# Mixing layer of a two-block model: columns reordered, small steps set between weight chunks, heads taken by pairs

## The reference

```python
def token_mix(x, w_in, w_out, ...):
    h = x @ w_in
    (nq, kc, vc, ks, vs, kw, vw, gl, u, gq, gk, gv, ga, gr) = jnp.split(h, split_pts, axis=-1)
    gates = jax.nn.sigmoid(gl).reshape(B, S, NSA_HEADS, 3)
    o_a = nsa_mixer(...)      # 8 heads of 64: attention over compressed, selected and window keys
    o_b = pool_mixer(u, pool_w, pool_scale)     # trailing means minus token, small product, scale
    o_c = gla_mixer(gq, gk, gv, ga, gr, ...)    # gated linear attention, 4 heads, chunks of 64
    return jnp.concatenate([o_a, o_b, o_c], axis=-1) @ w_out
```

## Time and profile before

| | us |
|---|---|
| median of 3 runs | 2589.47 |
| the runs | 2577.11, 2590.91, 2589.47 |
| the profiled execution, its own time | 2579.11 |
| span of the profiled execution | 2577.3 |
| TensorE busy (share) | 2478.0 (96%) |
| VectorE busy | 1514.1 (59%) |
| ACT busy | 1060.4 (41%) |
| GpSimd busy | 144.2 (6%) |
| mean granted clock of TensorE | 0.975 |

### The profile page before, as it was taken

The page is one execution under the profiler, slowest core; times in us unless marked ns, Lnnn a source line. Parts: engine busy times, 40 slices in busy tenths (PEclk is TensorE's granted clock), DMA queues, the critical chain, the costliest instruction groups (busy, mean ns, idle before and its releaser), DMA issues.

```text
span 2577.3 us, 43010 instructions
## 1 busy us (share of the span) xinstructions
PE 2478.0 (96%) x18918; PEld 2270.4 (88%) x18918; DVE 1514.1 (59%) x2062; ACT 1060.4 (41%) x1321; POOL 144.2 (6%) x174
## 2 busy tenths in 40 slices
PE   8999799999999899999999999999998999999998
PEld 8999579999999589989988989799897998998897
DVE  5456465564564555558655555755666555865654
ACT  4333344333334343336234344443455444633432
POOL 0001000000010000011110000100001000011000
PEclk9999699999999699999999999999999999999999
DMA  7569126556577045554225554455544555422553
GB/s 251 182 188 204 62 77 190 192 180 196 181 187 185 17 139 188 188 152 122 89 100 182 184 174 149 146 180 192 174 159 137 196 182 172 129 84 99 173 194 115
DMA packets 320810, 405.37 MB, mean 157 GB/s; under 512 B 48688, under 2 KB 281232, under 8 KB 320624
## 3 DMA queue, kind: packets, MB, share of 16 engines
q1 hardware_dynamic: 314960, 383.50, 47.2%
q0 software_dynamic: 5664, 19.13, 2.5%
HBM read 401.55 MB, written 1.05 MB: 156 GB/s over the span
## 4 chain that ended last, share of the span: by engine, by line
PE 86%; DVE 6%; ACT 3%; issue 2%; POOL 1%; DMA 1%; SPq 0%; DVEq 0%; POOLq 0%; ACTq 0%
PE ps L416 25%; PE ps L417 25%; PE ps L418 25%; PE ps L2233 2%; PE ps L707 1%; DVE w_lo L410 1%; ACT w_hi L403 1%; PE ps L1049 1%; DVE ws L1289 1%; DMA raw<-in_w_in 1%; DVE ws L1277 1%; PE ps L2275 1%; DVE ws L756 0%; DVE small L760 0%; PE ps L1061 0%
## 5 line engine op out<-in xcount | busy, mean ns | idle before, releaser
L410 DVE TENSOR_TENSOR w_lo<-raw,w_hi 128x2048 fp32r<-128x2048 f32 (+2 forms) x363 | 813.8, 2266 | 153.7 <-ACT w_hi L403 153.3
L403 ACT CAST w_hi<-raw 128x2048 fp32r<-128x2048 f32 (+2 forms) x363 | 685.5, 1889 | 498.0 <-PE ps L418 408.9
L416 PE MATMUL ps<-aT_hi,w_hi 128*128 128x256 f32 x2840 | 807.9, 284 | 0.2 <-DVE w_lo L410 0.2
L417 PE MATMUL ps<-aT_lo,w_hi 128*128 128x256 f32 x2840 | 804.1, 283 | 0.0
L418 PE MATMUL ps<-aT_hi,w_lo 128*128 128x256 f32 x2840 | 804.1, 283 | 0.0
L416 PEld LDWEIGHTS ps<-aT_hi,w_hi 128*128 128x128 f32 x2840 | 543.0, 191 | 5.1 <-DVE w_lo L410 0.4
L417 PEld LDWEIGHTS ps<-aT_lo,w_hi 128*128 128x128 f32 x2840 | 543.1, 191 | 3.7
L418 PEld LDWEIGHTS ps<-aT_hi,w_lo 128*128 128x128 f32 x2840 | 543.0, 191 | 0.5
L416 PE MATMUL ps<-w_hi,h_hi 128*128 128x512 f32 x928 | 363.4, 392 | 5.5 <-DVE h_lo L1566 4.2
L417 PE MATMUL ps<-w_lo,h_hi 128*128 128x512 f32 x928 | 362.4, 390 | 0.0
L418 PE MATMUL ps<-w_hi,h_lo 128*128 128x512 f32 x928 | 361.1, 389 | 0.0
(11 more groups left out here) (364 smaller groups left out, 2082.5 us busy)
## 6 DMA issues: line engine op xcount, KB each, us to landing
raw<-in_mlp_w SPq DMA_DIRECT2D x128, 1024.0 KB, 5.4
raw<-in_ffn_wd SPq DMA_DIRECT2D x44, 1024.0 KB, 4.9
raw<-in_ffn_wg SPq DMA_DIRECT2D x43, 1024.0 KB, 5.3
raw<-in_ffn_wu SPq DMA_DIRECT2D x43, 1024.0 KB, 5.3
raw<-in_gdn_w_in SPq DMA_DIRECT2D x32, 1024.0 KB, 5.7
raw<-in_mlstm_w_in SPq DMA_DIRECT2D x12, 1024.0 KB, 5.4
raw<-in_diff_w_in SPq DMA_DIRECT2D x12, 1024.0 KB, 5.2
raw<-in_w_in SPq DMA_DIRECT2D x8, 1024.0 KB, 5.8
```

The source lines that it names most:

```text
L403: nc.scalar.copy(used_part(hi_slot(n), n), used_part(raw[:, n % RAW, :], n)).then_inc(hi_ready, 1)
L410: nc.vector.tensor_tensor(used_part(lo_slot(n), n), used_part(raw[:, n % RAW, :], n), used_part(hi_slot(n), n).bitcast(F32), ALU.subtract) ...
L416: nc.tensor.matmul(dst, l_hi, r_hi, start=start, stop=False)
L417: nc.tensor.matmul(dst, l_hi, r_lo, start=False, stop=False)
```

## The change

Nothing outside the mixing layer changes. In it:

- **Order of columns.** After values and pool input come GLA keys with gates and decay input (chunk 2), GLA queries and keys (3), raw keys (4), raw values (5), GLA values (6), GLA output gate (7), keys (8), queries (9, 10). The row chunks for pool and GLA outputs come first, the two for head outputs last.
- **Small steps between chunks.** TensorE, ACT and VectorE each have the steps at fixed places: some between the two halves of a chunk, some between chunks. The splits of chunks stand among them.
- **GLA.** The first state is a masked copy, not a sum with a cleared tile; values inside and from before a chunk are summed in one PSUM bank, where a copy and an add stood; ACT takes the squares.
- **Heads by pairs.** scores(f) and values(f) take two heads with their matmuls in turn; ACT copies all 1024 turned columns, and VectorE none; four buffers of probabilities. One row chunk stands before the last transposes, one after the last values; the last two run together as before.

The diff, cut to its core (definitions of the steps that are only moved are left out):

```diff
+                for pieces in ([(NSA_VS, P), (NSA_VW, P)], [(POOL_U, 256)], [(GLA_K, P), (NSA_GATE, 24), (GLA_A, 16)], [(GLA_Q, 256)],
+                               twice(NSA_KC), twice(NSA_VC), [(GLA_V, 256)], [(GLA_R, 256)], [(NSA_KS, P), (NSA_KW, P)],
+                               heads(0), heads(128)):
+                    plan.append(column_pieces(wi, pieces))
...
-                plan += [mixed_row_pieces(wo, 0), mixed_row_pieces(wo, 256), row_pieces(wo, 512), row_pieces(wo, 768)]
+                plan += [row_pieces(wo, 512), row_pieces(wo, 768), mixed_row_pieces(wo, 0), mixed_row_pieces(wo, 256)]
...
+        def pool_means():
+            by_act(1)
+            pe.wait_ge(mix_landed.sem, 16 * MIX_LOADS * (l + 1))
...
+        def scores(f):
+            if f:
+                pe.wait_ge(peaked.sem, peaked.count(l, 2 * f - 1))
+            for k, (keys, more) in enumerate(((k_sel, N_CMP), (k_win, 0))):
+                for t in range(TT):
+                    for g in range(2):
+                        r = slice(64 * g, 64 * g + 64)
+                        o = ps[:, 2 * g + k, (more + P) * t:(more + P) + (more + SEQ) * t]
+                        last = nc.tensor.matmul(o, qT[r, f, t * P:(t + 1) * P], keys[r, 0:more + P * (t + 1)], start=True, stop=True)
...
+        tokens_product(pe, n0 + 2, 2, 168, between=pool_means)
+        by_act(0)
+        features_product(pe, n0 + 3, 0, between=decay_input)
+        pool_outputs()
+        features_product(pe, n0 + 4, 1, between=log_decays)
+        features_product(pe, n0 + 5, 2, between=decay_sums)
+        by_act(2)
+        tokens_product(pe, n0 + 6, 0)
+        compress_hidden()
+        gla_scores()
+        tokens_product(pe, n0 + 7, 1)
+        gla_states()
+        compressed()
+        features_product(pe, n0 + 8, 2)
+        gla_values()
+        features_product(pe, n0 + 9, 0)
+        pe.wait_ge(cmp_set.sem, cmp_set.count(l, 1))
...
+        features_product(pe, n0 + 10, 4, between=first_scores)
+        by_act(6)
+        for f in range(4):
+            if f < 3:
+                scores(f + 1)
+            turned_over(2 * f)
+            if f == 1:
+                gla_output_turned()
+            if f == 3:
+                pe.wait_ge(peaked.sem, peaked.count(l, 7))
+                rows(0, 2)
+            turned_over(2 * f + 1)
+            if f == 2:
+                pe.wait_ge(mixT_lo.sem, mixT_lo.count(l, 1))
+            values(f)
+        rows(1, 3)
...
     def mix_scalar(act, l):
...
+        split_high(act, n0 + 6)
+        act.wait_ge(ga_turned.sem, ga_turned.count(l, 0))
+        act.wait_ge(mix_set.sem, mix_set.count(l, 0))
+        nc.scalar.copy(ga_T[0:16, :], ps[0:16, 3, 0:SEQ]).then_inc(ga_set.sem, 1)
...
+        split_high(act, n0 + 13)
+        exps(0)
+        projected(10)
+        nc.scalar.copy(cols(0, 512, 1024), ps[:, 4, :]).then_inc(mix_act.sem, 1)
+        exps(1)
+        act.wait_ge(pool_scaled.sem, pool_scaled.count(l, 3))
+        output_high(4, pool_y)
+        for f in range(4):
+            copies(2 * f)
...
+            if f < 3:
+                exps(2 * f + 2)
+            copies(2 * f + 1)
+            if f < 3:
+                exps(2 * f + 3)
+            if f == 0:
+                split_high(act, n1 + 3)
...
     def mix_vector(dve, l):
...
+        split_low(dve, n0 + 13)
+        gla_output()
+        peaks(0)
+        peaks(1)
+        for f in range(4):
+            weights(2 * f)
+            if f < 3:
+                peaks(2 * f + 2)
+            weights(2 * f + 1)
+            if f < 3:
+                peaks(2 * f + 3)
+            if f == 0:
+                output_low(0, 4, pool_y)
+                split_low(dve, n1 + 3)
```

More of the change, by code:

```diff
@@ new lines, in log_decays, with decay_sums @@
+        def log_decays():
+            pe.wait_ge(ga_set.sem, ga_set.count(l, 0))
+            for t in range(TT):
+                last = nc.tensor.matmul(ps[:, 4, t * P:(t + 1) * P], ga_T[:, t * P:(t + 1) * P], wa2, start=True, stop=True)
+            last.then_inc(la_pre.sem, 1)
+        def decay_sums():
+            pe.wait_ge(la_set.sem, la_set.count(l, 0))
+            for t in range(TT):
+                s = slice(t * P, (t + 1) * P)
+                nc.tensor.matmul(ps[:, 3, s], la[:, s], consts[:, c_at["upto"]], start=True, stop=True)
+                last = nc.tensor.matmul(ps[:, 3, SEQ + t * P:SEQ + (t + 1) * P], consts[:, c_at["after"]], la[:, s],
+                                        start=True, stop=True)
+            last.then_inc(b_sum.sem, 1)
@@ new lines, in gla_values @@
+        def gla_values():
+            for t in range(TT):
+                for h in range(4):
+                    nc.tensor.matmul(ps[:, 5, t * 256 + 64 * h:t * 256 + 64 * h + 64], att[:, t, h * P:(h + 1) * P],
+                                     gv[:, t, 64 * h:64 * h + 64], start=(t == 0 and h == 0), stop=False)
+            for c in range(1, 4):
+                pe.wait_ge(s_set.sem, s_set.count(l, c - 1))
+                r = slice(64 * (c % 2), 64 * (c % 2) + 64)
+                last = nc.tensor.matmul(ps[r, 5, (c // 2) * 256:(c // 2 + 1) * 256], qtT[:, 64 * c:64 * c + 64], S_gla[:, c, :],
+                                        start=False, stop=c >= 2)
+            last.then_inc(gla_summed.sem, 1)
@@ L1067, in mix_tensor @@
-        for e in range(10):
-            if 1 <= e < 7:
-                scores(e + 1)
-            if 1 <= e <= 8:
-                turned_over(e - 1)
-            if e >= 2:
-                values(e - 2)
-        n1 = start["mix_out", l]
-        pair = lambda t, r: t[:, 2 * r:2 * r + 2, :].rearrange("p k s -> p (k s)")
-        for r in range(2):
-            pe.wait_ge(mixT_lo.sem, mixT_lo.count(l, 2 + r))
-            rows_product(pe, n1 + r, pair(aT_hi, r), pair(aT_lo, r), first=r == 0)
@@ L1160, in mix_scalar, with output_high @@
-        for r in range(3):
-            split_high(act, start["mix_out", l] + r + 3)
+            nc.scalar.copy(turned_probs(e).rearrange("p (b s) -> p b s", b=2), ps[:, 4:6, :]).then_inc(pT_act.sem, 1)
+        def output_high(k, src):
+            nc.scalar.copy(aT_hi[:, k:k + 2, :], src.rearrange("p (k s) -> p k s", s=SEQ)).then_inc(mixT_hi.sem, 1)
+        projected(0)
+        nc.scalar.copy(cols(1, 1024, 1536), ps[:, 0, :]).then_inc(mix_act.sem, 1)
+        projected(1)
+        nc.scalar.copy(cols(1, 1536, 2048), ps[:, 1, :]).then_inc(mix_act.sem, 1)
@@ L1315, in mix_vector @@
+        split_low(dve, n1 + 5)
         dve_steps[0] = ch.n
-        for r in range(3):
-            split_low(dve, start["mix_out", l] + r + 3)
     def window_view(bank, r):
```

540 lines of the change are left out of this document (252 added, 288 removed).

## The result

Four runs of the changed kernel gave 2547.76, 2547.37, 2536.74 and 2540.39 us, median 2543.88; beside them the kernel before had 2588.05. The ratio is 0.9839, 95% interval 0.9818 to 0.9859: about 42 us less. The prediction was 2547. The profiled execution took 2547.76 us, with a span of 2546.0 (before: 2579.11 and 2577.3), so 31.3 us of span are to be found.

What follows compares the result with a forecast made beforehand. TensorE, 86% of the chain, was taken as the bound, losing time to waits and low clock in the mixing layers. 2579.1 - 52.6 + 12 (clock) + 4 (shapes) = 2542.5, with the offset 2547 us; range 2522 to 2576.

Steps and rivals of the forecast that it cites:

- Nine chunks and small steps: Mixing layer's first stage: nine weight chunks 51.4 us as before, small steps between them 17.1 us at the upper clock.
- The load wait: In chunk 2, pool means wait for GpSimd's small loads: 3.1 us in layer 1, 2.6 in layer 2.
- Changes of shape: TensorE gaps where small steps meet full-size products: 2 us per layer, between 0 and 4; 4 us added in all.
- Pairs share the array: Two heads' scores and values run together on TensorE; without overlap each pair has 3.4 us more; no-overlap rival's chance 0.03.
- ACT busier than TensorE: Sign in the heads: per pair, ACT has 7.0 us of work, TensorE 5.6, so the bound moves to ACT.
- The heads: From chunk 10's end at 287.0 to 342.2, two row chunks included: 55.2 us at the upper clock in layer 1.
- the walk: Both layers' new engine programs followed in order with profiled durations: 137.7 and 137.3 us, 52.6 less together at the upper clock.
- The clock: In the heads, TensorE's clock falls in the first waits: 6 us per layer, 12 in all, half the full price.
- clock rival: Two rivals for the heads: clock stays up, 2535 us, chance 0.15; clock low through all pairs, 2560 us, chance 0.16.
- slower case: Low clock lasts from the first pair into the output row chunks, 5.46 us each for four: 2598 us, chance 0.04.
- late split: Queue rival's sign in the chunks: small steps delay ACT and VectorE, each 1.8 us late, 2584 us; chance 0.07.
- The offset: Added to the profiled-execution forecast: half of the 10.4 us by which the earlier median exceeded the profiled run.

Runs made afterwards that it cites:

- the three edits and the fillers: Changed kernel plus own pool-matrix signal, later n1+3 split, scores(1) ahead of by_act(6), and two unused matmuls ahead of transposes 1, 2, 3, 5: 2515.40 us, ratio 0.9734.
- the base: The changed kernel run again unaltered, against the kernel before: 2543.44 us, ratio 0.9853.
- Serial issue: Changed kernel with scores and values of each pair issued one head after the other: 2564.41 us, ratio 0.9923 to the kernel before.
- the fillers alone: Changed kernel plus two unused 512-column matmuls ahead of transposes 1, 2, 3 and 5 of each mixing layer: 2541.02 us, ratio 0.9848 to the kernel before.
- the run without it: Changed kernel with VectorE's split of n1+3 moved from ahead of weights(2) to ahead of its n1+4 split: 2540.78 us, ratio 0.9841 to the kernel before.
- the first trace: The profiled execution of the changed kernel, before the follow-up runs: 2547.76 us, span 2546.0.
- the three edits and no fillers: Changed kernel plus own pool-matrix signal, later n1+3 split, and scores(1) ahead of by_act(6): 2533.08 us, ratio 0.9807 to the kernel before.

## Why the prediction was right, step by step

**Nine chunks and small steps, 51.4 + 17.1 = 68.5 us at the upper clock: right.** With the load wait gone and the clock up (the three edits and the fillers) the stage takes 69.08 and 69.24 us, and TensorE is busy 68.5 and 68.6 of them. The 0.5 us are a short wait for VectorE.

**The load wait, 3.1 and 2.6 us: right as a place, too small.** 3.5 and 4.1 us; the last load lands 7.9 and 8.6 us after its issue instead of 7.5. What the step left out is the clock behind it: wait and clock together cost 8.8 us in the two layers. I had put the whole low clock into the heads.

**Changes of shape, 4 us: there, but not on top of the sum.** The changes are in the trace. Here is scores(0) inside chunk 10, from the base:

```profile
284.43 0.28 PE L410 MATMUL ps<-aT_hi,w_lo 128*128 128x256 f32 x1
284.64 1.63 PE L1026 MATMUL ps<-ws 64*128 64x143 f32 x16
286.20 0.38 PE L408 MATMUL ps<-aT_hi,w_hi 128*128 128x256 f32 x1
286.42 0.28 PE L409 MATMUL ps<-aT_lo,w_hi 128*128 128x256 f32 x1
```

Products follow each other at 0.12 us; here 0.21 lie between the last product and the first score, and 0.22 between the first product behind and the next. That is 0.1 us for each change. The chunk takes 7.50 us with the scores and 5.76 without, 1.74 where the sum had 1.45 for them. For ten such steps it comes to about 2 us a layer (an estimate from this one place), but the stage as a whole is 68.5 us, which the 17.1 us for the small steps already reach. Other steps were priced high enough to hold it: compression's first layer and the GLA scores take 5.4 us with their changes of shape, for 5.7 in the sum. So the separate 4 us were too much. The rule of the Trainium skill that the prediction weighed (TensorEngine Tiling (Array Packing), Key Properties), that a change of tiling mode drains the engine, is not contradicted: there is a gap at each change, and the rows do not show what makes it.

**Pairs share the array: right.** Serial issue costs 18 to 21 us. I had 3.4 us a pair, and the rows show 2.8. That the bound moves to ACT does not show: in layer 1's heads ACT is busy 29.4 us and TensorE 35.4, the row chunk and the half pace included, so the sign "ACT busier than TensorE" did not come.

**The heads, 55.2 us with both row chunks at the upper clock: nearly right in sum, and by errors that cancel.** In the trace with the fillers alone and clock 1.00, chunk 10's end to the end of rows 1 is 43.5 + 9.7 = 53.2 us; no trace has the heads at that clock without fillers. I forecast 5.3 us of wait ahead of scores(1), because of exps(0)'s table load; the table was loaded at 284.44, while ACT had nothing to do, and the wait is 3.1. I forecast 5.0 ahead of transposes 2, and it is 2.8. The cause that I named for the second, the split of n1+3, is shown by the run without it. Values and transposes of the other pairs wait a little more than in the walk.

**The clock, 12 us: right for the heads, short in sum.** For the heads, 49.9 and 50.3 us stand against 43.5 at clock 1.00 with fillers: 6.4 and 6.7 us, where I had 6 for each. Half of the full price was a choice between two bounds, not a working, so that it fits is luck in part. Behind the load wait the first trace has 1.5 us in layer 1 and 5.5 in layer 2 on top (TensorE's busy 70.0 and 74.0 us less 68.5). The profiled execution took 2547.8 where the sum was 2542.5, 5.3 more. Of these 3.2 lie outside the mixing layers. Inside them the two layers are 18.1 us above the sum at the upper clock (293.1 against 275.0), where I had allowed 16: the load wait is 1.9 larger, the clock behind it 7.0, and the heads to the end of rows 1 are 9.2 above the 110.4 of the walk (59.6 + 60.0), which is their clock less waits shorter than in the walk. Neither clock rival came: it was neither up in all the heads nor down in all of them. The row chunks behind the heads ran at 1.00. The slower case's mechanism did start in the row chunk inside the heads, whose first eight products in the base's layer 1 have its pace of 0.43 us:

```profile
331.35 0.63 PE L409 MATMUL ps<-w_lo,aT_hi 128*128 128x512 f32 x1
331.78 0.63 PE L410 MATMUL ps<-w_hi,aT_lo 128*128 128x512 f32 x1
```

The other sixteen are at 0.23, so it cost under 2 us. None of TensorE's waits in the chunks was for a late split.

**The offset, 4.5 us: wrong in sign.** Half of the 10.4 us between the profiled run and the median is 5.2, and 4.5 was added. The changed kernel's profiled run was above its median, not below. The profiled time came out 5.3 us above its sum and the median 3 below its own, 2543.9 against 2547: the places and the larger terms were right, but that the figure is so near is luck in part, since the clock behind the load wait (7 us) was missing and 4 us of shape changes and the offset stood in for it.

## What to carry to other kernels

Where TensorE stands in many short waits, price the clock with them. Shorten waits first: here the own signal for what is read first was worth 9 us, while shortening one wait inside the heads gave nothing that the times show, in one of the two cases because the next wait took it up. Then try a cheap matmul into a free bank in the waits that remain, only those longer than the filler. Read one stage's clock column in two traces of the same kernel before a microsecond of it is put down to an edit. A wait moved to an earlier place should be split by what each reader needs, even where the loads were never late before.

## What was not expected of the hardware

- The granted clock differs between executions of one program in the same stage: 0.91 and 0.98 over layer 2's chunks, worth about 4 us, and 0.73 against 0.79 in the heads, where 1.0 and 1.4 us lie between the two.
- Eight useless matmuls per layer, about 8 us of TensorE's time in waits, raised the heads from 0.75 to 1.00 and 0.96 and made them 6.1 and 4.5 us shorter. The heads still hold their 64 transposes per layer. The Trainium skill (TensorE: Matmul & The Clock Gate, Part 4: PE-mode transpose) says that the full clock does not engage for transposes. Here they do run at it: eight of a set start within 0.9 us at the upper clock and in 1.8 at the lower, so in this case the trace speaks against that sentence. Whether transposes alone would raise the clock, no run here shows, for other matmuls stand between the sets.
- The length of the longest wait does not tell whether the clock falls. Behind the same unfilled wait of 3.15 us it stayed up in layer 1 and fell in layer 2, in both traces that have fillers and this wait. With the three edits and no fillers no wait in the heads of layer 1 is longer than 2.3 us, and they ran at 0.75.
